# Layer 0 of a conditioned decoder step: one third of the conditioning projection ahead of the convolution, two thirds among its projections

## The chip, the cores and the metric

The kernel runs on one core of one Trainium2 chip. The time is device microseconds of one execution; each time shown is a median over the runs that are listed with it. The engines that matter here are PE (TensorE, matrix products), ACT (ScalarE), DVE (VectorE), POOL (GpSimd, which only issues transfers here) and SP (SyncE, which issues nearly all loads). They run their own instruction streams in order and meet at semaphores.

## What is computed

One inference step of a four-layer decoder trunk for 256 prompt tokens and 8 x 8 sample tokens (320 columns in all, model width 1024), all float32. Only layer 0 matters for the change:

```python
def adaln(c, w, b):
    mod = jax.nn.silu(c) @ w + b
    return jnp.split(mod[:, None, :], 6, axis=-1)

def modulate(x, g, shift, scale):
    return rms_norm(x, g) * (1 + scale) + shift
...
    sh1p, sc1p, g1p, sh2p, sc2p, g2p = adaln(c_prompt, ada_w[i], ada_b[i])
    hp = modulate(xp, norm1_g[i], sh1p, sc1p)
    yp, stp = conv_mixer(hp, ...)      # h @ w_in, a width-3 convolution with gates, @ w_out
    xp = xp + g1p * yp
    xp = xp + g2p * sq_relu_mlp(modulate(xp, norm2_g[i], sh2p, sc2p), mlp_w1[i], mlp_w2[i])
```

`ada_w` of a layer is 1024 x 6144. Its six blocks of 1024 columns are shift and scale of the first norm (sh1, sc1), the first gate (g1), shift and scale of the second norm (sh2, sc2) and the second gate (g2). The first norm needs sh1 and sc1 alone; g1 is needed when the convolution's output projection is added to x; sc2 and g2 are needed in the MLP. The other layers are windowed attention, pooling and latent attention over a paged cache, each followed by an MLP. Apart from y, the step returns the states, among them rolled copies of the attention windows (`out_swa_s`).

## The kernel before

Everything is written out by hand, engine by engine, with semaphores between them.

**Weights.** SP loads weight units of 1 MB (128 partitions x 2048 words) into a ring of four slots (`ring`, `load`, L421). Unit U may be loaded when unit U - 4 has been used (`unit_done`). For most phases each unit is split before use: ACT copies it to a rounded part `ring_hi` (`weights_hi`, L660, two halves), DVE subtracts to get the rest `ring_lo` in place (`weights_lo`, L1606), and PE runs three products per 128 x 128 block (hi x hi, hi x low of the input, low x hi). `conv_in` has 12 units of 48 such matmuls of 320 columns (L999); `conv_out` has 4 units of 16 plain float32 matmuls.

**The conditioning projection.** `ada_w` of a layer goes in three thirds r = 0, 1, 2 of eight units each. `ada_products(r, k)` (L1043) multiplies one unit by the 32 columns of `silu_c` into bank 5 or 6, in four matmuls of 512 columns; `ada_copy(r)` on ACT (L670) copies the bank out, `ada_turn(r)` on PE (L1052) transposes it with four matmuls into bank 7, and `ada_add(r)` on DVE (L1704) adds the bias and writes `mod`; `ada_scales` (L1713) turns the scale rows into (1 + scale) x gain. Third 0 holds sh1 and sc1, third 1 g1 and sh2, third 2 sc2 and g2. For layer 0 all 24 units come through the weight ring at the very start, ahead of the first norm. For layers 1 to 3 they come through a ring of their own of two slots (`ada_ring`, `ada_load`, L435), one unit behind each of 24 units of the MLP of the layer before.

**The first norm.** ACT squares x (L683), PE sums the squares with eight matmuls by ones into bank 4 (L1014), ACT takes the root (L685), DVE the reciprocal (L1577). Then for each pair of the eight chunks DVE multiplies (L1585) and treats the sample columns (L1593, L1594), ACT applies scale and shift to the prompt columns (L689) and makes `h_hi` (L695), DVE makes `h_lo` (L1581), and PE may start on that pair.

**The convolution.** The outputs of `conv_in` units 0 to 7 are copied out by ACT (L701). From unit 8 on DVE mixes: per chunk one group L1735 to L1749, eight chunks in all, 3.1 us each. PE waits for all eight (`conv_mixed`) before `conv_out`. DVE adds the output projection into x (L1612 to L1616, `mixer_update`), PE then turns the convolution's state (L961), ACT copies it out (L795) and goes on to the MLP.

**Rolled windows.** POOL issues 80 copies of up to 684 KB from `state_swa` to `out_swa_s`, DRAM to DRAM (`roll`, L326): 12 behind `conv_in`, 4 behind `conv_out`, 18 in layer 1, 8 + 16 in the projections and the prompt attention of layer 3, and 22 in the last MLP. The prompt attention's are each released by one head's products (`mlp_pv`).

Of the kernel before, what the change touches and what calls it, by code (L numbers as in the profile page):

```python
# [17 lines left out]
KD = D // P  # L18
# [29 lines left out]
NCH = {"ada": [0] * 24}  # L48
# [126 lines left out]
def build(nc, A, O):  # L175
    with ExitStack() as ctx:
# [237 lines left out]
        def _(sp):  # L414
# [12 lines left out]
            for u in range(24):  # L427
                load(u, u % RING, 1, SLOT, ada_rows_of(0, u // 8, u % 8), first=u < RING)

            def ada_load(l, x):  # L430

                y = 24 * (l - 1) + x
                if y >= 2:
                    sp.wait_ge(sem("ada_unit_done"), y - 1)
                sp.dma_start(ada_ring[:, x % 2, :].rearrange("p (k c) -> p k c", k=1), ada_rows_of(l, x // 8, x % 8))\  # L435
                  .then_inc(sem(f"ada_landed{x % 2}"), 16)

            def plain(phase, w, n, kc=KD, cols=256, col0=0):
                v = w.rearrange("(k p) n -> p k n", p=P)
                for u in range(n):  # L440
                    U = UNIT0[phase] + u
                    c = col0 + u * cols
                    width = min(cols, v.shape[2] - c)
                    load(U, U % RING, kc, width, v[:, :, c:c + width])

# [13 lines left out]
            plain("conv_in", A["conv_w_in"][0], 12)  # L459
            plain("conv_out", A["conv_w_out"][0], 4)  # L460
# [79 lines left out]
        def _(gp):  # L540
# [16 lines left out]
            roll_behind(0, "conv_in", 12)  # L557
            roll_behind(12, "conv_out", 4)
# [5 lines left out]
            roll_behind(16, "swa_qk", 12)  # L564
            roll_behind(28, "swa_v", 6)
# [25 lines left out]
            roll_behind(34, "mla_qa", 2)  # L591
            roll_behind(36, "mla_kva", 2)
            roll_behind(38, "mla_qb", 4)
# [4 lines left out]
            for i in range(16):  # L598
                gp.wait_ge(sem("mlp_pv"), i + 1)
                roll(42 + i)  # L600
# [17 lines left out]
        def _(act):  # L618
# [43 lines left out]
            def ada_copy(r):  # L662

                if r < 3:
                    act.wait_ge(sem("unit_done"), 8 * r + 8)
                else:
                    act.wait_ge(sem("ada_unit_done"), 8 * (r - 3) + 8)
                if r >= 2:
                    act.wait_ge(sem("ada_turned"), r - 1)
                act.activation(ada_rows[:, r % 2, :], bank[5 + r % 2][:, :], ACT.Copy).then_inc(sem("ada_copied"), 1)  # L670

            for r in range(3):
                ada_copy(r)
            weights_hi("conv_in", 0)
            weights_hi("conv_in", 1)

            def norm(ni, split=False):
# [7 lines left out]
                act.activation(rstd[:, 0, :], bank[4][:, 0:T], ACT.Sqrt, bias=tb("eps"), scale=1.0 / D).then_inc(sem("norm_std"), 1)  # L685
                for k in range(KD):
# [98 lines left out]
            norm(0, split=True)  # L785
# [5 lines left out]
            weights_hi("conv_in", 10)  # L791
            weights_hi("conv_in", 11)
            act.wait_ge(sem("conv_state_turned"), 1)
# [158 lines left out]
        def _(pe):  # L952
# [78 lines left out]
            def ada_products(r, k):  # L1031

                u = 8 * r + k
                if r < 3:
                    weights(u)
                    w = ring[:, u % RING, :]
                else:
                    pe.wait_ge(sem(f"ada_landed{k % 2}"), 16 * ((u - 24) // 2 + 1))
                    w = ada_ring[:, k % 2, :]
# [5 lines left out]
                mm.then_inc(sem("unit_done" if r < 3 else "ada_unit_done"), 1)  # L1045
# [78 lines left out]
            for r in range(3):  # L1124
                for k in range(KD):
                    ada_products(r, k)
                    if k == 2 and r:
                        ada_turn(r - 1)
            ada_turn(2)


            pe.wait_ge(sem("ada_read"), 5)
            norm(0, split=True)
            pairs("conv_in", 12, KD, ni=0)
            pe.wait_ge(sem("conv_mixed"), KD)
            pairs("conv_out", 4, KD, lambda k: cv_b[:, k, :])
            pe.wait_ge(sem("conv_state_ready"), 1)
# [428 lines left out]
        def _(dve):  # L1566
# [6 lines left out]
            def norm(ni, split=False):  # L1573
# [3 lines left out]
                own.link(dve.reciprocal(rstd[:, 0, :], rstd[:, 0, :]))  # L1577

# [128 lines left out]
            def ada_scales(l):  # L1707

                dve.wait_ge(sem("ada_read"), 3 * l + 5)
                for w in range(2):  # L1710
                    s = mod[:, mod_base(l, 3 * w + 1):mod_base(l, 3 * w + 1) + KD, :]
                    g = vcols((VEC_N2 if w else VEC_N1) + l * KD, KD).unsqueeze(2).to_broadcast([P, KD, 1 + NS])
                    ins = dve.scalar_tensor_tensor(s, s, 1.0, g, ALU.add, ALU.mult)  # L1713
                    own.link(ins) if w else own.mark(ins)
# [4 lines left out]
            for r in range(3):  # L1719
                ada_add(r)  # L1720
            ada_scales(0)


            weights_lo("conv_in", 0)
            weights_lo("conv_in", 1)
            norm(0, split=True)
            for u in range(2, 10):
                weights_lo("conv_in", u)
            for k in range(KD):
                if k in (2, 4):  # L1730
                    weights_lo("conv_in", 9 + k // 2)
                a = chunk_no("conv_in", 8 + k // 2, k % 2)
# [20 lines left out]
            mixer_update("conv_out", 0)  # L1753
            mlp(0)
# [341 lines left out]
```

## Time and profile before

| | us |
|---|---|
| median of three runs | 2438.51 |
| the three runs | 2429.34, 2438.51, 2442.95 |
| the profiled execution's own time | 2434.47 |
| its span | 2432.7 |
| PE busy in the span | 2135.9 (88%) |
| DVE busy | 1105.0 (45%) |
| ACT busy | 829.2 (34%) |
| read from HBM over the span | 392.01 MB |

The profile shows one execution. A row of the timeline gives start, duration, engine, line, operation, tile written and tiles read, shapes, and in brackets the idle time of the engine before it and what ended it. Lines are those of the kernel before; helpers such as `load` or `weights_hi` have one line for all their uses. A matmul of four-pass float32 shows as two records, so x8 under L1043 is one unit's four matmuls. PEclk is the granted TensorE clock as a share of 2.4 GHz.

### The profile page before, as it was taken

How to read it: one execution, taken by the hardware profiler on the slowest of the kernel's cores; microseconds unless marked ns; L12 is line 12 of the kernel's file. 1: busy time of each engine (PE TensorE's matmuls, PEld its weight loads, DVE VectorE, ACT ScalarE, POOL GpSimd, SP SyncE). 2: the span in 40 equal slices, each digit the busy share in tenths (PEclk: the TensorE clock that was granted, in tenths of full speed). 3: DMA queues.
4: the chain of work that ended last, by engine and by line, in shares of the span. 5: the costliest groups of instructions: out<-in, count | busy, mean ns of one | idle time of the engine just before them, and what ended most of it. 6: DMA issues, size and time to landing. Idle time of an engine off the chain costs nothing.

```text
span 2432.7 us, 33869 instructions
## 1 busy us (share of the span) xinstructions
PE 2135.9 (88%) x13570; PEld 1805.3 (74%) x13570; DVE 1105.0 (45%) x1760; ACT 829.2 (34%) x1445; POOL 54.0 (2%) x110
## 2 busy tenths in 40 slices
PE   4599799989968777999978999897899999889997
PEld 1297788879966555888867888863587777669997
DVE  1234554237815444553256542467533433335532
ACT  0230443135523332443224432343333333224421
POOL 0000000000010000000000000000100000000000
PEclk9799899999977898999989999997699999889999
DMA  7665377644560894477633776441501001026652
GB/s 281 256 228 197 133 246 263 217 141 170 203 216 24 238 280 127 156 248 263 201 98 122 246 263 224 146 165 61 183 20 44 22 22 43 1 69 225 242 212 74
DMA packets 230779, 399.45 MB, mean 164 GB/s; under 512 B 10184, under 2 KB 196335, under 8 KB 216689
## 3 DMA queue, kind: packets, MB, share of 16 engines
q1 hardware_dynamic: 224912, 332.69, 42.1%
q0 software_dynamic: 4576, 59.77, 6.3%
q10 hardware_dynamic: 1161, 5.11, 0.6%
q8 instruction: 100, 1.64, 0.3%
q14 instruction: 30, 0.25, 0.0%
HBM read 392.01 MB, written 59.76 MB: 186 GB/s over the span
## 4 chain that ended last, share of the span: by engine, by line
PE 77%; DVE 10%; DMA 6%; ACT 3%; issue 2%; SPq 1%; ACTq 0%; POOL 0%; DVEq 0%; POOLq 0%
PE bank L1069 37%; PE bank L999 11%; PE bank L1469 8%; PE bank L961 4%; PE bank L1043 3%; DVE rstd L1670 2%; PE bank L1161 2%; PE bank L1014 2%; DMA ring<-in_ada_w 2%; PE bank L1508 1%; PE bank L1478 1%; DMA work<-in_state_swa 1%; DMA ring<-in_mlp_w 1%; DVE hT L1585 1%; PE bank L1286 1%
## 5 line engine op out<-in xcount | busy, mean ns | idle before, releaser
L1606 DVE TENSOR_TENSOR ring_lo<-ring,ring_hi 128x1024 fp32r<-128x1024 f32 (+1 forms) x324 | 379.1, 1213 | 427.9 <-ACT ring_hi L660 427.8
L660 ACT ACTIVATE ring_hi<-ring 128x1024 fp32r<-128x1024 f32 (+1 forms) x324 | 322.8, 1046 | 452.2 <-PE bank L1069 185.8
L1069 PE MATMUL bank<-h_hi,ring_hi 128*128 128x320 f32 x1024 | 325.4, 318 | 27.8 <-DVE h_lo L1581 27.4
L1069 PE MATMUL bank<-hidden_hi,ring_hi 128*128 128x320 f32 x1024 | 322.9, 315 | 0.0
L1069 PE MATMUL bank<-h_lo,ring_hi 128*128 128x320 f32 x1024 | 319.2, 312 | 0.0
L1069 PE MATMUL bank<-hidden_lo,ring_hi 128*128 128x320 f32 x1024 | 318.5, 311 | 0.0
L1069 PE MATMUL bank<-h_hi,ring_lo 128*128 128x320 f32 x1024 | 318.5, 311 | 0.0
L1069 PE MATMUL bank<-hidden_hi,ring_lo 128*128 128x320 f32 x1024 | 318.5, 311 | 0.0
L961 PE MATMUL bank<-tab,work 128*128 128x128 f32 (+4 forms) x804 | 146.9, 323 | 116.8 <-DVE latents_lo L1992 17.5
L1069 PEld LDWEIGHTS bank<-h_hi,ring_hi 128*128 128x128 f32 x1024 | 195.2, 191 | 63.5 <-issue 60.7
L1069 PEld LDWEIGHTS bank<-hidden_hi,ring_hi 128*128 128x128 f32 x1024 | 194.6, 190 | 25.2 <-issue 25.2
L961 PEld LDWEIGHTS bank<-tab,work 128*128 128x128 f32 (+4 forms) x804 | 100.5, 158 | 151.5 <-issue 31.2
L1069 PEld LDWEIGHTS bank<-h_lo,ring_hi 128*128 128x128 f32 x1024 | 196.0, 191 | 0.0
L1069 PEld LDWEIGHTS bank<-h_hi,ring_lo 128*128 128x128 f32 x1024 | 195.4, 191 | 0.0
L1069 PEld LDWEIGHTS bank<-hidden_lo,ring_hi 128*128 128x128 f32 x1024 | 194.6, 190 | 0.0
L1069 PEld LDWEIGHTS bank<-hidden_hi,ring_lo 128*128 128x128 f32 x1024 | 194.3, 190 | 0.0
L1469 PE MATMUL bank<-ring_hi,latents_hi 128*128 128x512 f32 x512 | 172.7, 420 | 0.0
L999 PE MATMUL bank<-h_hi,ring_hi 128*128 128x320 f32 (+1 forms) x432 | 141.4, 327 | 20.6 <-DVE h_lo L1581 20.3
L1998 DVE TENSOR_REDUCE work<-work 128x8 f32<-128x1024 f32 x64 | 78.1, 1220 | 154.8 <-ACT work L909 154.8
L999 PE MATMUL bank<-h_lo,ring_hi 128*128 128x320 f32 (+1 forms) x432 | 136.9, 317 | 0.0
L999 PE MATMUL bank<-h_hi,ring_lo 128*128 128x320 f32 (+1 forms) x432 | 136.4, 316 | 0.0
L1642 DVE TENSOR_TENSOR work<-work x128 | 63.0, 492 | 141.5 <-ACT work L774 141.5
(242 smaller groups left out, 3075.4 us busy)
## 6 DMA issues: line engine op xcount, KB each, us to landing
ring<-in_mlp_w SPq DMA_DIRECT2D x128, 1024.0 KB, 7.6
work<-in_ada_w SPq DMA_DIRECT2D x72, 1024.0 KB, 5.2
out_swa_s<-in_state_swa POOLq DMA_DIRECT2D x40, 684.0 KB, 6.0
ring<-in_ada_w SPq DMA_DIRECT2D x24, 1024.0 KB, 8.8
work<-in_state_swa SPq DMA_DIRECT2D x80, 256.0 KB, 10.5
ring<-in_swa_w_qkv SPq DMA_DIRECT2D x18, 1024.0 KB, 6.6
work<-in_state_swa SPq DMA_DIRECT2D x16, 1024.0 KB, 9.8
out_swa_s<-in_state_swa POOLq DMA_DIRECT2D x24, 672.0 KB, 5.9
```

The source lines that it names most:

```text
L660: act.activation(ring_hi[:, place, part], ring[:, s, part], ACT.Copy).then_inc(sem("weights_hi"), 1)
L961: return pe.transpose(dst, src, ident[0:m, 0:m])
L999: mm = pe.matmul(bank[a % 4][0:m, 0:n], w[:, k, col:col + m], x(k), start=i == j == 0, stop=i == len(ks) - 1 and j == len(terms) - 1)
L1014: mm = pe.matmul(bank[4][:, 0:T], ones, hT[:, k, :], start=k == 0, stop=k == KD - 1)
L1043: mm = pe.matmul(bank[5 + r % 2][32 * j:32 * j + 32, :], silu_c[:, k, :], w[:, j * 512:(j + 1) * 512], start=k == 0, stop=k == KD - 1)
L1069: mm = pe.matmul(bank[a % 4][:, 0:T], w[:, k, :], x(k), start=first and k == 0 and j == 0, stop=last and k == KD - 1 and j == 2)
L1161: mm = pe.matmul(bank[a % 4][0:m, 0:256], x[:, k, t * P:t * P + m], w[:, k, :], start=k == j == 0, stop=k == KD - 1 and j == 2)
L1469: mm = pe.matmul(bank[2 * (x % 2) + i][:, :], lT_parts[y][:, c, x, :], kvb_parts[z][:, c, 512 * i:512 * (i + 1)], start=c == y == z == 0, ...
L1606: dve.tensor_tensor(ring_lo[:, s, part], ring[:, s, part], ring_hi[:, place, part], ALU.subtract)\
L1642: dve.tensor_tensor(raw, raw, raw, ALU.mult).then_inc(sem("hidden_squared"), 1)
L1670: own.link(dve.reciprocal(r, r))
L1998: dve.tensor_reduce(md_ss[:, j - 1, :], md_sq[:, :].rearrange("p (h d) -> p h d", h=H), AX_X, ALU.add)\
```

## The change

The first norm's squares and their sum go ahead of all conditioning products. Of the 24 conditioning units of layer 0 only the eight of third 0 still come through the weight ring at the start. The other sixteen come through `ada_ring`, and PE multiplies one behind each of the twelve `conv_in` units and two behind each of the first two `conv_out` units; `ada_turn(1)` stands behind unit 9 of `conv_in`, `ada_turn(2)` behind the last `conv_out` unit. On ACT the split of `conv_in` unit 0 stands ahead of `ada_copy(0)`, and that of unit 1 behind the norm instead of ahead of it; DVE follows suit. Sixteen rolled copies leave the convolution; all later ones move up, and sixteen are now issued in the decode part of layer 3, one behind every fourth page of keys (`md_keys`).

```diff
-NCH = {"ada": [0] * 24}
+NCH = {"ada": [0] * 8}
...
-            for u in range(24):
-                load(u, u % RING, 1, SLOT, ada_rows_of(0, u // 8, u % 8), first=u < RING)
+            for u in range(8):
+                load(u, u % RING, 1, SLOT, ada_rows_of(0, 0, u), first=u < RING)
...
-                y = 24 * (l - 1) + x
+                y = 24 * l + x - 8
                 if y >= 2:
                     sp.wait_ge(sem("ada_unit_done"), y - 1)
                 sp.dma_start(ada_ring[:, x % 2, :].rearrange("p (k c) -> p k c", k=1), ada_rows_of(l, x // 8, x % 8))\
...
-            def plain(phase, w, n, kc=KD, cols=256, col0=0):
+            def plain(phase, w, n, kc=KD, cols=256, col0=0, behind=lambda u: ()):
...
                     load(U, U % RING, kc, width, v[:, :, c:c + width])
+                    for x in behind(u):
+                        ada_load(0, x)
...
-            plain("conv_in", A["conv_w_in"][0], 12)
-            plain("conv_out", A["conv_w_out"][0], 4)
+            plain("conv_in", A["conv_w_in"][0], 12, behind=lambda u: (8 + u - 3,) if u >= 3 else ())
+            plain("conv_out", A["conv_w_out"][0], 4, behind=lambda u: ((17,), (18,), (19, 20), (21, 22, 23))[u])
...
-            roll_behind(0, "conv_in", 12)
-            roll_behind(12, "conv_out", 4)
...
-            roll_behind(16, "swa_qk", 12)
-            roll_behind(28, "swa_v", 6)
...
-            roll_behind(38, "mla_qb", 4)
+            roll_behind(18, "mla_qa", 2)
+            roll_behind(20, "mla_kva", 2)
...
             for i in range(16):
                 gp.wait_ge(sem("mlp_pv"), i + 1)
+                roll(26 + i)
+            for i in range(16):
+                gp.wait_ge(sem("md_keys"), 4 * i + 3)
                 roll(42 + i)
             roll_behind(58, "mlp1_3", 16)
             roll_behind(74, "mlp2_3", NS * len(ROLL) - 74)
...
-                if r < 3:
-                    act.wait_ge(sem("unit_done"), 8 * r + 8)
+                if r < 1:
+                    act.wait_ge(sem("unit_done"), 8)
                 else:
-                    act.wait_ge(sem("ada_unit_done"), 8 * (r - 3) + 8)
+                    act.wait_ge(sem("ada_unit_done"), 8 * r)
                 if r >= 2:
                     act.wait_ge(sem("ada_turned"), r - 1)
                 act.activation(ada_rows[:, r % 2, :], bank[5 + r % 2][:, :], ACT.Copy).then_inc(sem("ada_copied"), 1)
...
                 act.wait_ge(sem("norm_sum"), ni + 1)
                 act.activation(rstd[:, 0, :], bank[4][:, 0:T], ACT.Sqrt, bias=tb("eps"), scale=1.0 / D).then_inc(sem("norm_std"), 1)
+                if between:
+                    between()
...
-            norm(0, split=True)
+            def front():
+                weights_hi("conv_in", 0)
+                ada_copy(0)
+
+            norm(0, split=True, between=front)
+            weights_hi("conv_in", 1)
             for u in range(8):
                 for c in range(2):
                     k = 2 * u + c
                     copy_chunk("conv_in", u, c, (cv_b if k < KD else cv_c)[:, k % KD, :])
                 weights_hi("conv_in", u + 2)
             weights_hi("conv_in", 10)
+            ada_copy(1)
             weights_hi("conv_in", 11)
+            ada_copy(2)
             act.wait_ge(sem("conv_state_turned"), 1)
...
-                if r < 3:
+                if r < 1:
                     weights(u)
                     w = ring[:, u % RING, :]
                 else:
-                    pe.wait_ge(sem(f"ada_landed{k % 2}"), 16 * ((u - 24) // 2 + 1))
+                    pe.wait_ge(sem(f"ada_landed{k % 2}"), 16 * ((u - 8) // 2 + 1))
                     w = ada_ring[:, k % 2, :]
                 if k == 0 and r >= 2:
...
-                mm.then_inc(sem("unit_done" if r < 3 else "ada_unit_done"), 1)
...
-            for r in range(3):
-                for k in range(KD):
-                    ada_products(r, k)
-                    if k == 2 and r:
-                        ada_turn(r - 1)
-            ada_turn(2)
-
-
+            pe.wait_ge(sem("ada_read"), 2)
+            norm(0, split=True)
+            for k in range(KD):
+                ada_products(0, k)
+            ada_turn(0)
+
+            def ada_behind_in(u):
+                ada_products(1 + u // 8, u % 8)
+                if u == 9:
+                    ada_turn(1)
+
+            def ada_behind_out(u):
+                if u < 2:
+                    ada_products(2, 4 + 2 * u)
+                    ada_products(2, 5 + 2 * u)
+                if u == 3:
+                    ada_turn(2)
+
+            pairs("conv_in", 12, KD, ni=0, each=ada_behind_in)
+            pe.wait_ge(sem("conv_mixed"), KD)
+            pairs("conv_out", 4, KD, lambda k: cv_b[:, k, :], each=ada_behind_out)
+            pe.wait_ge(sem("conv_state_ready"), 1)
             pe.wait_ge(sem("ada_read"), 5)
-            norm(0, split=True)
-            pairs("conv_in", 12, KD, ni=0)
-            pe.wait_ge(sem("conv_mixed"), KD)
-            pairs("conv_out", 4, KD, lambda k: cv_b[:, k, :])
-            pe.wait_ge(sem("conv_state_ready"), 1)
...
                 dve.wait_ge(sem("norm_std"), ni + 1)
                 own.link(dve.reciprocal(rstd[:, 0, :], rstd[:, 0, :]))
+                if between:
+                    between()
...
-            for r in range(3):
-                ada_add(r)
-            ada_scales(0)
-
-
-            weights_lo("conv_in", 0)
+            def front():
+                weights_lo("conv_in", 0)
+                ada_add(0)
+                ada_scales(0, (0,))
+
+            norm(0, split=True, between=front)
             weights_lo("conv_in", 1)
-            norm(0, split=True)
             for u in range(2, 10):
                 weights_lo("conv_in", u)
             for k in range(KD):
                 if k in (2, 4):
                     weights_lo("conv_in", 9 + k // 2)
+                if k == 4:
+                    ada_add(1)
                 a = chunk_no("conv_in", 8 + k // 2, k % 2)
                 wait_read(dve, chunk_no("conv_in", 4 + k // 2, k % 2))
                 wait_chunk(dve, "conv_in", 8 + k // 2, k % 2)
...
             mixer_update("conv_out", 0)
+            ada_add(2)
+            ada_scales(0, (1,))
```

PE, from the end of the transposes of x (L968 in the changed kernel; lines shift by 7 on PE). Before, all conditioning products come first (the pattern runs on for 24 units):

```order
L961 MATMUL bank<-tab,work 128x64
L1043 MATMUL bank<-ring,silu_c 32x512 [waits x_ready,weights_landed0,x_copied,silu_ready]
L1043 MATMUL bank<-ring,silu_c 32x512 x3
L1043 MATMUL bank<-ring,silu_c 32x512 [waits weights_landed1]
L1043 MATMUL bank<-ring,silu_c 32x512 x3
```

In the changed kernel the sums of squares come first (L1021), then eight units (L1050), of which the last is shown, the transpose (L1059) and the first `conv_in` unit (L1006):

```order
L1021 MATMUL bank<-hT,tab 128x320 [waits ada_read,x_ready,squares,x_copied,silu_ready]
L1021 MATMUL bank<-hT,tab 128x320
...
L1050 MATMUL bank<-ring,silu_c 32x512 [waits weights_landed3]
L1050 MATMUL bank<-ring,silu_c 32x512 x3
L1059 MATMUL bank<-tab,work 128x36 [waits ada_read,ada_copied]
L1059 MATMUL bank<-tab,work 128x36 x3
L1006 MATMUL bank<-h_hi,ring_hi 128x320 [waits h_split,weights_split]
```

The sum moved past sixteen units that have left this place, and past eight that stay.

ACT of the changed kernel, from the squares to the split of `conv_in` unit 1 (L663 is `weights_hi`, L673 `ada_copy`, L689 and L695 the norm's first pair):

```order
L681 ACTIVATE hT<-xT 128x640 [waits x_ready] x4
L683 ACT_TABLE_LOAD
L683 ACTIVATE rstd<-bank,tab 128x320 [waits norm_sum]
L663 ACTIVATE ring_hi<-ring 128x1024 [waits unit_done,weights_landed0]
L663 ACTIVATE ring_hi<-ring 128x1024
L673 ACTIVATE work<-bank 128x512 [waits unit_done]
L689 ACTIVATE hT<-hT,mod 128x256 [waits normed]
...
L695 ACTIVATE h_hi<-hT 128x640 [waits h_sample,h_prompt]
L663 ACTIVATE ring_hi<-ring 128x1024 [waits unit_done,weights_landed1]
```

The copy of the third now stands behind the split of a weight unit; before it stood ahead of both splits.

SP of the changed kernel, from the start to the third conditioning unit in the convolution:

```order
L421 DMA ring<-in_ada_w 128x2048 x4
L421 DMA ring<-in_ada_w 128x2048 [waits unit_done] x4
L421 DMA ring<-in_conv_w_in 128x8x256 [waits unit_done] x4
L435 DMA work<-in_ada_w 128x2048
L421 DMA ring<-in_conv_w_in 128x8x256 [waits unit_done]
L435 DMA work<-in_ada_w 128x2048
L421 DMA ring<-in_conv_w_in 128x8x256 [waits unit_done]
L435 DMA work<-in_ada_w 128x2048 [waits ada_unit_done]
```

Each conditioning load stands right behind the load of the `conv_in` unit that waits for the fourth unit before it; before, the twelve `conv_in` loads followed one another.

## Rows read from the trace of the kernel before

**Rows 1.** The page: shares of the chain that ended last.
```profile
PE 77%; DVE 10%; DMA 6%; ACT 3%; issue 2%; SPq 1%; ACTq 0%; POOL 0%; DVEq 0%; POOLq 0%
```

**Rows 2.** Windows: length, busy time and instructions per engine, clock, DMA share, GB/s.
```profile
100.00:125.00 25.00, 18.13 (x68) 14.84 (x67) 10.98 (x18) 10.56 (x18) 0.00 (x1) 0.70 0.01 3
125.00:150.00 25.00, 25.00 (x172) 25.00 (x172) 9.45 (x8) 10.81 (x16) 2.02 (x4) 1.00 0.75 264
```

**Rows 3.** Timeline of the front, all engines: from the first product to `conv_in`.
```profile
33.91 6.49 PE L1043 MATMUL bank<-ring,silu_c 128*32 128x512 f32 x32 [0.79 <-DVE xT L1696]
...
50.54 1.93 PE L1043 MATMUL bank<-ring,silu_c 128*32 128x512 f32 x8 [1.56 <-DMA ring<-in_ada_w]
52.55 0.60 ACT L670 ACTIVATE work<-bank 128x512 f32<-128x512 f32 x1 [36.39 <-PE bank L1043]
...
83.98 90.39 SPq L421 DMA_DIRECT2D ring<-in_conv_w_in  x12
...
90.42 1.93 PE L1043 MATMUL bank<-ring,silu_c 128*32 128x512 f32 x8 [0.67 <-DMA ring<-in_ada_w]
...
93.07 1.92 PE L1052 MATMUL bank<-tab,work 128*128 128x36 f32 x8 [0.72 <-ACT work L670]
93.42 2.00 ACT L660 ACTIVATE ring_hi<-ring 128x1024 fp32r<-128x1024 f32 x2 [0.39 <-DMA ring<-in_conv_w_in]
95.03 0.31 DVE L1704 TENSOR_TENSOR mod<-bank,vec 128x144 f32<-128x144 f32 x1 [14.72 <-PE bank L1052]
...
98.34 2.60 ACT L683 ACTIVATE hT<-xT 128x640 f32<-128x640 f32 x4
...
99.20 7.20 PE L1014 MATMUL bank<-hT,tab 128*128 128x320 f32 x16 [4.20 <-ACT hT L683]
...
109.18 0.82 DVE L1585 TENSOR_TENSOR hT<-xT,rstd 128x640 f32<-128x640 f32 x1
...
112.93 0.60 PE L999 MATMUL bank<-h_hi,ring_hi 128*128 128x320 f32 x1 [6.53 <-DVE h_lo L1581]
```

**Rows 4.** Chain that ended last, layer 0's MLP: start, length, what.
```profile
296.04 1.00 PE bank L1043 x8
297.04 7.23 PE bank L1069 x48
...
436.89 1.01 PE bank L1052 x8
```

**Rows 5.** End of `conv_in` (POOL's copy behind its last unit), DVE's last chunk.
```profile
202.43 0.49 POOL L326 DMA_DIRECT2D out_swa_s<-in_state_swa  x1 [6.55 <-PE bank L999]
...
203.52 0.41 DVE L1735 TENSOR_TENSOR work<-work,bank 128x256 f32<-128x256 f32 x1
```

**Rows 6.** The same chain: all of `conv_out`.
```profile
206.63 36.41 PE bank L999 x128
```

**Rows 7.** DVE behind the first two chunks of `conv_out`.
```profile
212.94 0.48 DVE L1612 SCALAR_TENSOR_TENSOR xT<-bank,mod,xT 128x256 f32<-128x256 f32 x1 [6.14 <-PE bank L999]
...
217.24 0.48 DVE L1612 SCALAR_TENSOR_TENSOR xT<-bank,mod,xT 128x256 f32<-128x256 f32 x1 [3.43 <-PE bank L999]
```

**Rows 8.** SP's issues at 275 us and their landing (last number: us to landing).
```profile
274.95 0.37 SPq L421 DMA_DIRECT2D ring<-in_mlp_w  x1
275.36 0.58 SPq L435 DMA_DIRECT2D work<-in_ada_w  x1
...
ring<-in_mlp_w SPq DMA_DIRECT2D x1, 1024.0 KB, 5.7
work<-in_ada_w SPq DMA_DIRECT2D x1, 1024.0 KB, 7.7
```

**Rows 9.** The conditioning load issued at 243.49 us, with a rolled copy beside it.
```profile
work<-in_ada_w SPq DMA_DIRECT2D x1, 1024.0 KB, 10.5
```

**Rows 10.** DMA issues of layer 3's decode: the pages.
```profile
work<-in_cache_mla SPq DMA_DIRECT2D x64, 160.0 KB, 2.2
```

**Rows 11.** The window of the decode part of layer 3.
```profile
1760.00:2110.00 350.00, 330.06 (x1821) 271.84 (x1821) 138.95 (x222) 129.74 (x294) 0.00 (x0) 0.96 0.10 27
```

More of the change, by code:

```diff
@@ L561, in _ @@
             gp.dma_start(O["conv_s"].rearrange("a n r d -> (a n r) d"), cv_out[2:18, :]).then_inc(sem("conv_rows_stored"), 16)
-            roll_behind(16, "swa_qk", 12)
-            roll_behind(28, "swa_v", 6)
+            roll_behind(0, "swa_qk", 12)
+            roll_behind(12, "swa_v", 6)
             wait_banks(gp, "swa_out")
@@ L589, in _ @@
             gp.dma_start(O["pool_s"][0, :, HIST - SS:HIST], pl_out[0:TS, 1, :]).then_inc(sem("pool_rows_stored"), 16)
-            roll_behind(34, "mla_qa", 2)
-            roll_behind(36, "mla_kva", 2)
-            roll_behind(38, "mla_qb", 4)
+            roll_behind(18, "mla_qa", 2)
+            roll_behind(20, "mla_kva", 2)
+            roll_behind(22, "mla_qb", 4)
             gp.wait_ge(sem("latent_tok"), 3)
@@ L670, in ada_copy, with norm @@
                 act.activation(ada_rows[:, r % 2, :], bank[5 + r % 2][:, :], ACT.Copy).then_inc(sem("ada_copied"), 1)
-            for r in range(3):
[L673 to L677, printed above, removed]
+            def norm(ni, split=False, between=None):
                 l, w = ni // 2, ni % 2
@@ L1044, in ada_products @@
                                    start=k == 0, stop=k == KD - 1)
-                mm.then_inc(sem("unit_done" if r < 3 else "ada_unit_done"), 1)
+                mm.then_inc(sem("unit_done" if r < 1 else "ada_unit_done"), 1)
             def ada_turn(r):
@@ L1571, in seq, with norm @@
                 return ap.rearrange("p (n s) -> p n s", s=SS)
-            def norm(ni, split=False):
+            def norm(ni, split=False, between=None):
                 l, w = ni // 2, ni % 2
@@ L1705, in ada_add, with ada_scales @@
                    .then_inc(sem("ada_read"), 1)
-            def ada_scales(l):
-                dve.wait_ge(sem("ada_read"), 3 * l + 5)
-                for w in range(2):
+            def ada_scales(l, which=(0, 1)):
+                dve.wait_ge(sem("ada_read"), 3 * l + (5 if 1 in which else 3))
+                for w in which:
                     s = mod[:, mod_base(l, 3 * w + 1):mod_base(l, 3 * w + 1) + KD, :]
@@ L1713, in ada_scales @@
                     ins = dve.scalar_tensor_tensor(s, s, 1.0, g, ALU.add, ALU.mult)
-                    own.link(ins) if w else own.mark(ins)
+                    own.link(ins) if w == which[-1] else own.mark(ins)
                 if l == 2:
@@ L1717, in ada_scales @@
                     own.link(dve.tensor_tensor(g, g, vcols(VEC_POOL, KD).unsqueeze(2).to_broadcast([P, KD, 1 + NS]), ALU.mult))
-            for r in range(3):
-                ada_add(r)
-            ada_scales(0)
-            weights_lo("conv_in", 0)
+            def front():
[3 more added lines that the diff above has]
+            norm(0, split=True, between=front)
             weights_lo("conv_in", 1)
-            norm(0, split=True)
             for u in range(2, 10):
```

## The prediction

> **What bounds the kernel now.** Read the page's chain first [rows 1]: three quarters of the span end on PE, so the question for any stretch is whether PE works or waits. Then the windows [rows 2]. Between 125 and 150 us PE is busy without a gap at the full clock; between 100 and 125 us it is busy 18 of 25 us at a granted clock of 0.70, a mix of the 1.2 and the 2.4 GHz level, with the transfers idle. So the front is loose and the convolution is PE-bound. The front timeline [rows 3] says why. The first products begin at 33.91 us and take 6.49 us for the four units that have landed (x32 records, eight per unit); from then on PE waits for each 1 MB unit. The eighth unit starts at 50.54 us and the 24th at 90.42 us: sixteen units in 39.9 us, 2.49 us each, all of it transfer time. Behind them comes a serial piece of 22.5 us until the first `conv_in` matmul at 112.93 us: turn, bias, four splits on DVE, squares, sum, root, reciprocal, first pair of the norm.
>
> All times below are of the profiled execution (2434.47 us, span 2432.7); it lies 4.0 us, 0.17%, under the median of 2438.51 us. A measurement of this kernel can tell about 0.5% from no change (12.2 us); the three runs of before alone spread over 13.6 us.
>
> **The front.** I follow the new order with durations of before.
> - The squares need only x and an idle ACT: from 33.7 us on, the first pair done 0.65 us later (2.60 us for four) [rows 3]. PE's sum is eight float32 matmuls of 320 columns. At their old place they took 7.20 us in a stretch of clock 0.70 [rows 2, 3]; the same eight as a `conv_out` chunk take 217.24 - 212.94 = 4.30 us [rows 7]. Dense transposes run right ahead of the new place, and PE is idle for under 2 us in between, so I take 4.3 us; the other end is 7.2. The first product moves from 33.91 to 38.7 us: **4.8 us later**. Root and reciprocal lie beside products and transfers and cost nothing; what covers them is the wait for units 4 to 7.
> - Units 4 to 7 are released by the first products, so their landings move by the same 4.8 us: the eighth starts at 55.3 and ends at 57.2 us.
> - SP now has `conv_in` unit 0 behind the eighth. At the old end of the queue it landed 93.42 - 90.42 = 3.0 us behind the last conditioning unit [rows 3], so at 58.3 us. ACT splits it (2.00 us) before it copies the third (0.60 us): that order puts the copy at 60.4 instead of 57.3 us, a new wait of 3.1 us. Copy until 61.0; from the turn to the end of the bias row 95.03 + 0.31 - 93.07 = 2.3 us, and 0.4 us for one scale and its handoff: the norm's first multiplication can start at 63.8 us instead of 109.18 [rows 3]. **Gain 45.4 us**, and the first `conv_in` matmul moves from 112.93 to 67.5 us.
> - Unit 1's split now follows the norm on ACT: norm done near 72, ACT until 74.2, DVE until about 76 us. PE's unit 0 starts at 67.5 us, and it takes over 10 us as before, since it starts at the low clock behind single norm pairs; so this costs nothing.
>
> **The convolution.** In the MLP of layer 0 one unit with one conditioning unit behind it takes 1.00 + 7.23 = 8.23 us [rows 4]; a `conv_in` unit alone takes 7.04 us (the distance of POOL's copies, 6.55 idle + 0.49 [rows 5]). One conditioning unit so costs 1.19 us, a turn 1.01 us [rows 4]. Eleven stand between units of `conv_in`, with one turn: **+14.1 us**. The twelfth falls into the wait for DVE. That wait was 206.63 - 202.4 = 4.2 us, because DVE came to the last chunk at 203.52, 1.1 us late [rows 5, 6]; with PE slower by a sixth DVE keeps up and only its 3.1 us for the last chunk remain: **-1.1 us**. Four units in `conv_out` add 4.8 us. Behind it PE has a turn (1.0), and the state's transposes now wait for the bias of that turn (0.3, with 0.1 for the handoffs); ACT's state copies, the splits for the MLP and the second norm are queued behind: **+6.2 us** in all. The first chunk of `conv_out` took 6.3 us against 4.30 for the second [rows 6, 7], since PE had come out of 4.2 us of idleness at the low level; now a product unit shortens this idleness to 2 us. That saves between 0 and 2.0 us; I take **-1.0**.
>
> **The transfers beside it.** This is the place to look at hardest. The conditioning unit that PE needs behind `conv_in` unit j + 1 is loaded when unit j ends, behind a 1 MB weight load on the same queue. PE needs it one distance later, 8.23 us. Nearest row: such a pair, with nothing beside it, landed its second part 0.41 + 7.7 = 8.1 us after the first issue [rows 8]. That just fits; for scatter **+0.3 us**. With a rolled copy beside it the second part took 10.5 us [rows 9], 10.9 from the first issue; the change takes those copies away from here, so I stay with the row without one. Their removal gains nothing by itself: PE was already full [rows 2].
>
> The Trainium skill, "DMA: Bandwidth & Descriptors", section on the anatomy of one DMA, gives 2.0 us plus bytes at 436 GB/s per transfer; by that, as an estimate, the pair of 2 MiB would be there after 6.8 us, the slack would be 1.4 us and the +0.3 would be 0. The row's 8.1 us is the slower one and decides here.
>
> **The rolled copies.** Sixteen now run in layer 3's decode part, 350 us with a DMA share of 0.10 and 27 GB/s [rows 11]; a page lands in 2.2 us [rows 10] and is asked for about one sequence, some 40 us, ahead. Cost 0. Without that lead each could cost what a copy adds to a load (10.5 - 7.7 = 2.8 us [rows 8, 9]): at most 45 us.
>
> **Sum.** -45.4 + 14.1 - 1.1 + 6.2 - 1.0 + 0.3 = **-26.9 us**: the profiled execution would be 2408 us, the median 2411 us. Of 39.9 us of transfer taken out of the front, about 19 come back as PE time.
>
> **The rivals.**
> - *The conditioning loads pace the convolution, mildly.* If the pair lands after 9.3 us, near midway between the rows with and without a copy, each of eleven units waits 1.1 us: +12, so -15 and 2423 us. For it: the slack is 0.1 us, and only one unit of lead is left. Against: a good part of the present load there (DMA share 0.75 [rows 2]) is rolled copies, which go. Chance 0.13.
> - *The same, fully: slower than before.* It decides from a landing of 8.23 + 26.9/11 = 10.7 us on. The copy row's 10.9 is over it. `conv_in` unit 0, with others queued ahead, landed 93.42 - 83.98 = 9.4 us after its issue [rows 3]; with 2.49 us for a second transfer this is 11.9 us, 3.7 us late each time, +40 us, so +13 and 2452 us. Against: at 84 us the queue was several units deep, here it is empty each time. Chance 0.04.
> - *The rolled copies cost in the decode part.* If each of the sixteen delays PE by 1.9 us, two thirds of the bound above, the gain is gone (+3, 2442 us). PE is busy 330 of 350 us there [rows 11], so late pages would show in full; the lead speaks against. Chance 0.03.
> - *The front does not shrink as said*: the sum at the low clock (+2.9), and units 1 and 2 wait for splits that ACT now makes behind the norm, two of 2.0 + 1.2 us and a landing of 3 us bare, 9 us: -15, 2423 us. Chance 0.05.
> - *More than said*: `conv_out` starts at the full clock (-1.0), the order of split and copy costs nothing (-3.1), the start of `conv_in` is less broken up (-2): -33, 2405 us. Chance 0.09.
>
> **How the numbers follow.** The forecast has 0.66; its own range is 2403 to 2419 us (the terms' ends give -34 to -20, and the median of a few runs 2 us either way). Faster by over 0.5% means under 2426.3 us: the forecast, the better case, the mild pacing but for its worst part, most of the fourth: 0.88. Within 0.5%: 0.08. Slower: 0.04. The range from 2401 to 2425 us takes in the better case, the forecast and the milder half of the two cases at 2423, and leaves out the slow ones.
>
> **What would show it.** Right: the first `conv_in` matmul near 67.5 us; the sum of squares from 34.4 to 38.7 us; 8.2 us between ends of `conv_in` units; its end near 171, `conv_out` from 174 to 214 us; the decode part as long as before. Wrong: PE at L1050 waiting for `ada_w` for over 1 us per unit in `conv_in` (pacing); page loads over 2.2 us with PE waiting for them (rolled copies); ACT's split of unit 1 ending after PE's unit 0.

## The result, and the profile after

| | before | changed |
|---|---|---|
| median of eight runs each, us | 2440.70 | 2415.23 |
| lowest to highest | 2424.78 to 2448.17 | 2403.17 to 2422.02 |
| profiled execution, us | 2434.47 | 2403.17 |
| its span | 2432.7 | 2401.4 |
| PE busy | 2135.9 | 2124.0 |

The ratio is 0.990, with a 95% interval from 0.9873 to 0.9926: the medians differ by 25.5 us, and the interval allows 18 to 31 us. The forecast was 26.9 us, 2411 us, with a range from 2401 to 2425 us. The two profiled executions differ by 31.3 us; where the other 6 come from is told below, and they are not the change's.

The page of the changed kernel, its chain that ended last, reads as before [rows 1], with PE and ACT one point up each and transfers one point down:

```profile
span 2401.4 us, 33870 instructions
...
PE 78%; DVE 10%; DMA 5%; ACT 4%; issue 2%; SPq 1%; ACTq 0%; POOL 0%; DVEq 0%; POOLq 0%
```

The front of the changed kernel in its timeline (same columns as [rows 3], which it answers; L1021 is the sum, L1050 a conditioning unit, L1059 its turn, L1603 the norm's first multiplication, L1006 `conv_in`):

```profile
34.55 6.80 PE L1021 MATMUL bank<-hT,tab 128*128 128x320 f32 x16 [1.44 <-ACT hT L681]
...
41.28 3.64 PE L1050 MATMUL bank<-ring,silu_c 128*32 128x512 f32 x32
...
55.81 1.94 PE L1050 MATMUL bank<-ring,silu_c 128*32 128x512 f32 x8 [0.58 <-DMA ring<-in_ada_w]
58.80 2.00 ACT L663 ACTIVATE ring_hi<-ring 128x1024 fp32r<-128x1024 f32 x2 [16.88 <-DMA ring<-in_conv_w_in]
...
60.70 0.58 ACT L673 ACTIVATE work<-bank 128x512 f32<-128x512 f32 x1
...
61.33 1.93 PE L1059 MATMUL bank<-tab,work 128*128 128x36 f32 x8 [3.58 <-ACT work L673]
63.30 0.31 DVE L1722 TENSOR_TENSOR mod<-bank,vec 128x144 f32<-128x144 f32 x1 [0.97 <-PE bank L1059]
...
63.91 0.82 DVE L1603 TENSOR_TENSOR hT<-xT,rstd 128x640 f32<-128x640 f32 x1
...
67.65 0.61 PE L1006 MATMUL bank<-h_hi,ring_hi 128*128 128x320 f32 x1 [4.39 <-DVE h_lo L1599]
...
73.24 2.36 DVE L1624 TENSOR_TENSOR ring_lo<-ring,ring_hi 128x1024 fp32r<-128x1024 f32 x2
77.97 1.07 PE L1050 MATMUL bank<-work,silu_c 128*32 128x512 f32 x8
```

The norm starts at 63.91 instead of 109.18 us and `conv_in` at 67.65 instead of 112.93: 45.3 us. Unit 1's split on DVE is done at 75.60, before PE ends unit 0 at 77.97.

The chain through the convolution (start, length, what), which answers [rows 4 to 6]:

```profile
88.44 7.24 PE bank L1006 x48
95.68 0.99 PE bank L1050 x8
96.68 7.23 PE bank L1006 x48
...
120.81 8.59 DMA work<-in_ada_w
...
129.44 1.06 PE bank L1050 x8
...
175.64 10.55 PE bank L1006 x32
186.19 1.85 PE bank L1050 x16
188.05 8.81 PE bank L1006 x32
```

One unit with its conditioning unit takes 8.23 us. In three places PE waits for a conditioning load, for 1.11, 0.85 and 0.79 us; the second of them is for the load issued at 120.81. `conv_in` ends at 172.4 us (202.4 before [rows 5]), `conv_out` starts at 175.64 (206.63 [rows 6]). So 30 of the 45.3 us are left when `conv_in` ends, 31.0 at `conv_out`, and 25.4 at the sum of the second norm, which starts at 224.04 us instead of 249.48.

### The profile page after: what moved, and what is told of

The parts are those of the page before. It is cut to its first block, busy times and chain, and to the rows that moved or that the text cites. A ratio compares the mean times of both kernels' runs of the same rounds, so it can differ in the third digit from the quotient of the medians.

```text
span 2401.4 us, 33870 instructions
## 1 busy us (share of the span) xinstructions
PE 2124.0 (88%) x13570; PEld 1799.5 (75%) x13570; DVE 1105.6 (46%) x1760; ACT 828.5 (35%) x1445; POOL 54.0 (2%) x110
## 3 DMA queue, kind: packets, MB, share of 16 engines
HBM read 392.01 MB, written 59.76 MB: 188 GB/s over the span
## 4 chain that ended last, share of the span: by engine, by line
PE 78%; DVE 10%; DMA 5%; ACT 4%; issue 2%; SPq 1%; ACTq 0%; POOL 0%; DVEq 0%; POOLq 0%
PE bank L1076 37%; PE bank L1006 11%; PE bank L1485 8%; PE bank L968 4%; PE bank L1050 3%; DVE rstd L1688 2%; PE bank L1177 2%; PE bank L1021 2%; PE bank L1524 1%; PE bank L1494 1%; DMA work<-in_ada_w 1%; DMA ring<-in_mlp_w 1%; DVE hT L1603 1%; PE bank L1302 1%; PE bank L1496 1%
## 5 line engine op out<-in xcount | busy, mean ns | idle before, releaser
L663 ACT ACTIVATE ring_hi<-ring 128x1024 fp32r<-128x1024 f32 (+1 forms) x324 | 322.8, 1046 | 468.1 <-PE bank L1076 191.9
L968 PE MATMUL bank<-tab,work 128*128 128x128 f32 (+4 forms) x804 | 147.1, 324 | 116.3 <-DMA pages_sb<-in_page_table 14.9
L968 PEld LDWEIGHTS bank<-tab,work 128*128 128x128 f32 (+4 forms) x804 | 100.8, 159 | 151.6 <-issue 38.1
L1006 PE MATMUL bank<-h_hi,ring_hi 128*128 128x320 f32 (+1 forms) x432 | 142.4, 330 | 18.5 <-DVE h_lo L1599 18.2
L1006 PE MATMUL bank<-h_lo,ring_hi 128*128 128x320 f32 (+1 forms) x432 | 136.9, 317 | 0.0
L1006 PE MATMUL bank<-h_hi,ring_lo 128*128 128x320 f32 (+1 forms) x432 | 136.4, 316 | 0.0
```

The costliest lines, as they stand in the source:

```text
L663: act.activation(ring_hi[:, place, part], ring[:, s, part], ACT.Copy).then_inc(sem("weights_hi"), 1)
L968: return pe.transpose(dst, src, ident[0:m, 0:m])
L1006: mm = pe.matmul(bank[a % 4][0:m, 0:n], w[:, k, col:col + m], x(k), start=i == j == 0, stop=i == len(ks) - 1 and j == len(terms) - 1)
```

## The experiments

Each ran with the kernel before on the same chip; the ratio is to that kernel. Stretches are of each run's own profile.

| run | what is changed | ratio (95% interval) |
|---|---|---|
| changed kernel | | 0.990 (0.9873 to 0.9926) |
| e1 | rolled copies back behind the convolution | 0.9932 (0.9907 to 0.9957) |
| e2 | conditioning loads one unit earlier | 0.988 (0.985 to 0.991) |
| e3 | ACT's copy ahead of the split | 0.9881 (0.9859 to 0.9902) |
| e4 | four products ahead of the sum | 0.9875 (0.9848 to 0.9901) |
| e5 | kernel before, copies moved away | 0.9986 (0.9964 to 1.0008) |
| e6 | kernel before, sums ahead | 0.9981 (0.9959 to 1.0003) |
| e7 | e2, e4 and e9 together | 0.9862 (0.9834 to 0.989) |
| e8 | the two loads of a pair swapped | 0.99 (0.9865 to 0.9935) |
| e9 | e3, with DVE's order too | one run, 2408.28 us |
| e10 | one third in front; sums, copy and splits in their old order | 0.9909 (0.9875 to 0.9944) |

**e1, the rolled copies back.** In the changed kernel:

```diff
+            roll_behind(0, "conv_in", 12)
+            roll_behind(12, "conv_out", 4)
             gp.wait_ge(sem("conv_state_out"), 2)
...
                 gp.wait_ge(sem("mlp_pv"), i + 1)
-                roll(26 + i)
-            for i in range(16):
-                gp.wait_ge(sem("md_keys"), 4 * i + 3)
                 roll(42 + i)
```

The copies in between are numbered as in the kernel before.

> The changed kernel, with the sixteen rolled copies back behind the convolution's units, as before the change; all else is left. Theory (transfers pace the conditioning units once a copy runs beside them): the pair of loads lands 10.9 us after the first issue instead of 8.1 to 9.3, PE waits some 2.7 us at each of eleven conditioning units of conv_in, conv_in gets 25 to 30 us longer, and nearly the whole gain is gone: ratio to before 0.998 to 1.003. Rival (the landing has slack, the copies could have stayed): conv_in gets at most 5 us longer, ratio 0.990 to 0.993, and moving the copies was needless. Decode part of layer 3: same length either way.

`conv_in` from the end of unit 0 to that of unit 11 takes 107.3 us (78.12 to 185.46) instead of 94.4 (78.07 to 172.44): 13 us, half of what the theory said and well over its rival's 5. The time tells less: the ratio of 0.9932 lies below the theory's 0.998 and at the upper end of the rival's range, and its interval overlaps that of the changed kernel. First the landings between 75 and 170 us (last number), of the changed kernel:

```profile
work<-in_ada_w SPq DMA_DIRECT2D x12, 1024.0 KB, 7.8
ring<-in_conv_w_in SPq DMA_DIRECT2D x8, 1024.0 KB, 5.3
```

and of e1:

```profile
work<-in_ada_w SPq DMA_DIRECT2D x10, 1024.0 KB, 10.1
ring<-in_conv_w_in SPq DMA_DIRECT2D x8, 1024.0 KB, 6.8
```

The size of one landing was nearly right: 10.1 + 0.41 = 10.5 us from the first issue against 10.9 forecast. The number of waits was wrong. SP's timeline of e1 shows it; each row is the issue at the end of one unit:

```profile
78.12 0.37 SPq L421 DMA_DIRECT2D ring<-in_conv_w_in  x1
...
86.35 0.37 SPq L421 DMA_DIRECT2D ring<-in_conv_w_in  x1
...
98.45 0.37 SPq L421 DMA_DIRECT2D ring<-in_conv_w_in  x1
...
106.67 0.37 SPq L421 DMA_DIRECT2D ring<-in_conv_w_in  x1
```

The distances go 8.23, 12.10, 8.22. The pair for the next product is issued at a unit's end, before PE waits for the present one; so the wait is lead for the next pair, which then arrives in time. In all PE waited six times instead of eleven: 2.21, 2.57, 1.05, 1.22, 2.37 and 1.42 us, together 10.8 us against 2.75 us in the changed kernel. The rest of the 13 us is clock. Behind the first wait the granted clock was 0.50, the lower of its two levels; the products took 1.94 instead of 1.06 us and the next unit 7.95 instead of 7.23. The other two waits of over 2 us were followed by the same, which makes some 4.6 us for the three together; behind the three of 1.05 to 1.42 us the products took 1.07 us.

**e2, one unit of lead more.**

```diff
-            plain("conv_in", A["conv_w_in"][0], 12, behind=lambda u: (8 + u - 3,) if u >= 3 else ())
-            plain("conv_out", A["conv_w_out"][0], 4, behind=lambda u: ((17,), (18,), (19, 20), (21, 22, 23))[u])
+            plain("conv_in", A["conv_w_in"][0], 12, behind=lambda u: () if u < 3 else (8, 9) if u == 3 else (8 + u - 2,))
+            plain("conv_out", A["conv_w_out"][0], 4, behind=lambda u: ((18,), (19,), (20,), (21, 22, 23))[u])
```

> The changed kernel, with each conditioning load of the convolution issued one unit earlier (two loads behind conv_in unit 3, then one more ahead), so that PE has two units of lead instead of one. Theory (the three waits of about 1 us in conv_in are the pair landing later than 8.2 us): no wait for ada_w at the products behind conv_in, conv_in 3 us shorter, time 3 us less than the changed kernel, which the time alone cannot show. Rival (the waits come from the transfers' total rate, not from the lead): the waits stay or move to the ring weights, conv_in as long as now.

The theory holds. No product in `conv_in` waits for its weights; from the end of unit 0 to that of unit 11 it is 91.4 us (78.70 to 170.10) instead of 94.4; ten of the eleven distances are 8.2 us, the one with the turn is 9.1. The chain of e2, where the changed kernel has its first wait:

```profile
78.67 1.00 PE bank L1050 x8
79.67 7.24 PE bank L1006 x48
86.91 1.00 PE bank L1050 x8
87.91 7.23 PE bank L1006 x48
```

**e8, the order within the pair.** The conditioning load ahead of the weight load, at the same moment:

```diff
+                    if len(behind(u)) == 1:
+                        sp.wait_ge(sem("unit_done"), U - RING + 1)
+                        ada_load(0, behind(u)[0])
                     load(U, U % RING, kc, width, v[:, :, c:c + width])
-                    for x in behind(u):
-                        ada_load(0, x)
+                    if len(behind(u)) > 1:
+                        for x in behind(u):
+                            ada_load(0, x)
```

> The changed kernel, with the two loads behind each conv_in unit swapped in SP's queue (conditioning unit first, weight unit second), issued at the same moment as before. Theory (one queue serves them in order, the conditioning unit is late because the weight unit stands ahead of it): the conditioning unit lands after 5.2 us, as it does where the MLP issues it first, the weight unit after about 8; no wait at the products in conv_in, 3 us less than the changed kernel. Rival (the two share the engines evenly): both land after about 8 us in either order, the waits stay.

The waits are gone here too, with one unit of lead as in the changed kernel; from the end of unit 0 to that of unit 11 it is 91.4 us as in e2, and the ratio cannot show these 3 us. The landings of e8 between 75 and 170 us:

```profile
work<-in_ada_w SPq DMA_DIRECT2D x12, 1024.0 KB, 5.0
ring<-in_conv_w_in SPq DMA_DIRECT2D x8, 1024.0 KB, 7.5
```

5.0 and 7.5 us instead of 7.8 and 5.3: the load issued first is served first. The Trainium skill, "DMA: Bandwidth & Descriptors", section on queues, rings and completion order, says that a ring's descriptors are consumed in order; these two rows agree. So e1, e2 and e8 settle what the three waits are: a landing up to 1.1 us behind the need, because it stands behind a load that nobody is short of.

**e3 and e9, split and copy.**

```diff
             def front():
-                weights_hi("conv_in", 0)
                 ada_copy(0)
+                weights_hi("conv_in", 0)
```

> The changed kernel, with ACT copying the first third's products ahead of the split of conv_in unit 0, and DVE adding bias and scale ahead of its half of that split. Theory of the prediction (the order costs a wait of 3.1 us): the norm's first multiplication starts 3 us earlier, near 61 us. Rival (the landing of conv_in unit 0 at 58.8 us sets the end, the copy stood in its shadow): it starts only 1 to 1.6 us earlier, near 62.5 us, right behind DVE's half of the split.

This text speaks of DVE's order too; the kernel that ran had the lines above alone, and DVE's order was left. e9 then moved `weights_lo("conv_in", 0)` behind `ada_scales(0, (0,))` on DVE as well.

> The changed kernel, with the copy of the first third ahead of the split of conv_in unit 0 on ACT, and bias and scale ahead of DVE's half of it. The run e3 moved ACT's copy alone. Theory (the landing of conv_in unit 0 and its two-step split set the norm's start): first multiplication 3.4 to 3.6 us after that landing, 0.6 us better than e3's 4.05 us and 1.6 us better than the changed kernel's 5.1. Theory of the prediction (the order costs 3.1 us): 2.0 us after the landing.

From the landing of `conv_in` unit 0 (start of its split) to the norm's first multiplication it is 63.91 - 58.80 = 5.1 us in the changed kernel, 61.89 - 57.84 = 4.05 in e3, 62.49 - 59.02 = 3.47 in e9. The rival holds: what the order costs is 1.1 us (e3) to 1.6 us (e9, one execution), not 3.1. In e9 the copy is made at 57.76 and the scales are ready at 60.2, and DVE's split still holds the norm until 62.49. What sets the end is the landing and its two-step split.

**e4, products ahead of the sum.**

```diff
+            for k in range(RING):
+                ada_products(0, k)
             norm(0, split=True)
-            for k in range(KD):
+            for k in range(RING, KD):
                 ada_products(0, k)
```

> The changed kernel, with the products of the four landed conditioning units ahead of the sum of squares instead of behind it; the other four behind it. Theory (what the sum costs is that it holds back the release of the four ring slots): SP issues the fifth load at 36 us instead of 42.4, everything up to the norm moves 5 to 6.5 us ahead, first conv_in matmul near 62 us instead of 67.6; ratio to before 0.987 to 0.988. Rival (root and reciprocal then come too late, or the sum delays the fifth unit's products and with them conv_in unit 0's load): less than 3 us gained.

The theory holds. The chain of e4:

```profile
33.66 5.53 PE bank L1050 x32
39.19 4.50 PE bank L1021 x16
43.70 1.04 PE bank L1050 x8
```

The sum now lies in the wait for the fifth unit; `conv_in` unit 0 lands at 52.2 instead of 58.8 us, and the first `conv_in` matmul is at 61.03, 6.6 us earlier. The ratio, 0.9875, fits that and cannot be told from 0.990 by itself. (The second norm's sum starts 9.7 us earlier than in the changed kernel, at 214.37; 1.7 of these us are a first `conv_out` unit that came out at the full clock, see below.)

**e5 and e6, two parts of the change alone**, in the kernel before. e5 moves the rolled copies as the change does. e6 puts squares, sum, root and reciprocal ahead of all 24 units (`norm(0, split=True, between=front)` on ACT and DVE, with the three thirds and both splits in `front`).

> The kernel before, with one part of the change: the sixteen rolled copies leave the convolution, the later ones move up, sixteen run in the decode part of layer 3. Theory (the copies lay in cover at both places): no change, ratio 0.998 to 1.002, conv_in 7.04 us per unit as before, the decode part's key products as long as before (343 us from first to last). Rival (their removal frees PE or the ring in the convolution, so part of the gain is theirs): ratio 0.995 or less. Other rival (they slow the pages): over 1.003.

> The kernel before, with one part of the change: squares, sum, root and reciprocal of the first norm ahead of all 24 conditioning units, which all stay in front. Theory (the sum holds back the release of the ring's slots by 6.5 us, and what leaves the tail is the 8.7 us from the squares to the reciprocal): net 2 us gained, norm's first multiplication near 107 us instead of 109.2, not to be seen in the time (0.997 to 1.001). Rival (the sums ahead are a large part of the 45 us): 8 us or more gained, 0.996 or less, norm near 101 us.

e5: no change that can be told, as the theory said; its interval runs from 9 us faster to 2 us slower. The key products of the decode part (first and last start), before, changed and e5:

```profile
L1469 PEld LDWEIGHTS bank<-ring_hi,latents_hi x512: 186/188/338, 1763.5 to 2106.8; 128*128 128x128 f32 x171
```

```profile
L1485 PEld LDWEIGHTS bank<-ring_hi,latents_hi x512: 186/188/338, 1732.2 to 2075.6; 128*128 128x128 f32 x171
```

```profile
L1470 PEld LDWEIGHTS bank<-ring_hi,latents_hi x512: 186/188/338, 1768.9 to 2112.2; 128*128 128x128 f32 x171
```

343.3, 343.4 and 343.3 us: sixteen copies more in this part cost nothing there. From the first `conv_in` matmul to `conv_out` e5 takes 93.6 us (111.8 to 205.37), the kernel before 93.7, so the copies had not slowed PE in the old convolution either.

e6: 4.7 us, since `conv_in` starts at 108.22 instead of 112.93 us; more than the 2 expected, less than the rival's 8. The ratio, 0.9981, cannot be told from 1.

**e10, the short front with the sums at their old place.**

```diff
-            norm(0, split=True, between=front)
+            ada_copy(0)
+            weights_hi("conv_in", 0)
             weights_hi("conv_in", 1)
+            norm(0, split=True)
```

This is ACT. PE's `norm(0, split=True)` goes behind `ada_turn(0)`, and DVE's splits go behind its scales and ahead of the norm.

> The changed kernel, with the first norm's squares and sum at their old place behind the conditioning units and the splits of conv_in units 0 and 1; one third in front and two thirds beside the convolution as changed. It tells how the 45.3 us of the front divide. Theory (the eight units in front carry nearly all of it): norm's first multiplication near 69 us, 5 us later than in the changed kernel, first conv_in matmul near 73 us; ratio to before 0.990 to 0.993. Rival (only with the sums ahead does the short front pay): 10 us later or more, ratio 0.994 or over.

First multiplication at 68.81, first `conv_in` matmul at 72.55 us, ratio 0.9909. So of the 45.3 us of the front 40.4 come from the sixteen units that left. The other 4.9 are all of the new order together: the sums ahead and unit 1's split behind the norm, less what the split ahead of the copy costs (1.1 to 1.6 us by e3 and e9). e6, which moves only the sums in the kernel before, gives 4.7.

**e7, three of these edits together.** e2, e4 and e9 in one kernel.

> The changed kernel with the three edits of the runs before together: products of the four landed units ahead of the sum of squares, ACT's copy and DVE's bias and scale ahead of the split of conv_in unit 0, conditioning loads one unit earlier. Expected if they add: first conv_in matmul near 60 us (67.7 in the changed kernel), no wait for ada_w in conv_in, 10 us less than the changed kernel, ratio to before 0.984 to 0.987. If the ring weights or ACT become the bound of conv_in's first units: first matmul at 60 us but unit 1 waiting, and ratio 0.988.

First `conv_in` matmul at 59.76 us, 7.9 earlier than in the changed kernel; no wait in `conv_in`, which ends at 161.9 instead of 172.4 us. The ratio is 0.9862, the lowest of all, within the 0.984 to 0.987 expected, though its interval overlaps the changed kernel's. It cannot be told from e4 either, whose ratio is 0.9875 and whose median is 2408.5 us. The 10.5 us are in the trace; the medians of 2409.5 and 2415.2 us, taken on different occasions, show 6 of them, the two ratios 9. That e7 is faster than the changed kernel is likely, and not shown by the times.

## Why the prediction was right

*Front.* 45.4 us forecast, 45.3 measured; norm at 63.8, measured 63.91. That it agrees to 0.1 us is luck in part: two terms inside were off and stood against each other. The sum took 6.80, not 4.30 us, nearly the other end that was kept (5.94 to 7.39 us in the other runs that have it first). The four units behind it took 3.64 us, not the 6.49 of [rows 3], so the eighth unit started at 55.81 against 55.3. The step that failed here is "so I take 4.3 us", with its ground that dense transposes run right ahead. e4 puts the units first, and there they take 5.53 us and the sum 4.50: whatever comes first in this stretch runs slowly.

*Split ahead of copy.* Rightly carried through the sum, wrongly priced as a new wait of 3.1 us: most of the copy's delay stood in the shadow of a landing, and only 1.1 to 1.6 us of it could be had back (e3, e9).

*Convolution.* 8.23 us per unit forecast and measured; 1.19 us per conditioning unit is that less 7.04. Unit 0 took 10.4 us (67.65 to 78.07) where it took 12.1 before (112.93 to 125.00, where POOL issues its first copy behind `conv_in`). This 1.6 us was in no term of the sum; only the rival *More than said* named it, with 2 us. The wait for DVE is 175.64 - 172.42 = 3.2 us, forecast 3.1. The turn, the bias and the state's transposes behind `conv_out` came as forecast. The four units there cost 3.7 us, not 4.8, and the clock term was 0, not -1.0: the first unit took 10.55 us against 8.81 for the second. In e1 and e4, after the same idle time of 2.23 us, it took 8.88. So this term goes one way or the other from execution to execution, and what decides it was not found.

*Transfers.* Rightly named as the place to look; +0.3 forecast, 3.0 measured (94.4 against e2's 91.4 us), in three waits. Of all terms of the sum behind the front this is the one most mis-sized. The pair lands 8.2 us after the first issue in the middle, which is the need itself, and up to 9.3. The row at 8.1 us was one landing; its scatter was the term. The estimate from the figures of the Trainium skill, 6.8 us, was too low by 1.4; the skill gives them for a DMA on the software path, while the page of the profile has SP's loads on `q1 hardware_dynamic`.

*The slower rival* had the right mechanism and the wrong price. It charged each unit with a lateness; e1 shows 10.5 us landings costing 13 us, because a wait is lead for the next pair. By the same argument 11.9 us would not have cost 40; no run tried that.

*Rolled copies.* 0 forecast; in the decode part 0 measured (e5), in the whole time nothing that can be told. The move was still needed: with the copies in the convolution `conv_in` is 13 us longer, half of the gain (e1); the two ratios say a third, with intervals that overlap.

*Sum.* -45.3 in front, then 14.1 for the units and a turn, 2.8 of waits, -1.6 for unit 0, -1.0 at DVE's wait, 0.4 in `conv_out`'s own matmuls, 3.7 for its units and 1.5 behind it: -25.4 us at the second norm, forecast 26.9. So the two terms that were missed in `conv_in`, 2.5 us of waits and 1.6 us at unit 0, stood against each other too. That the medians say 25.5 is closer than their interval can promise. That the profiled pair shows 31.3 comes later, from pieces that take longer in one execution than in the other after idle stretches that both kernels have. Chain of the kernel before:

```profile
460.94 9.62 PE bank L1069 x48
...
535.30 7.62 PE bank L1014 x16
```

and of the changed kernel, the same two pieces:

```profile
434.74 8.85 PE bank L1076 x48
...
508.32 4.59 PE bank L1021 x16
```

The same sum of eight matmuls takes 7.62 us in one execution and 4.59 in the other, and nothing of the change is near: these two pieces are 3.8 of the 5.9 us. Pieces like these may also be part of why runs of the changed kernel spread over 19 us; this was not tried.

## What to carry to other kernels

If only a third of a projection is needed at first, it is worth loading alone: what lay bare as transfer came back as PE time at less than half (16 units: 39.9 us bare, 1.2 or less each beside other work). When a load is placed one step ahead of its use, compare its landing, counted from the first load in the queue at that moment, with the step's length; if they are equal, issue it one step earlier or put it ahead of the load that has slack. Before pricing a wait on one engine, look at whether a landing ends behind it anyway.

## What the runs showed of the hardware

The clock column can read full where matmuls run at half the rate. This is the changed kernel's sum, first in windows of 1 us (busy shares of the engines, and the granted clock as the third number from the end; the counts take in records that only reach into a window), then by PE's weight loads, one per record:

```profile
36.00:37.00 1.00, 1.00 (x3) 0.61 (x3) 0.00 (x0) 0.98 (x2) 0.00 (x0) 1.00 0.00 0
...
40.00:41.00 1.00, 1.00 (x6) 0.60 (x4) 0.00 (x0) 0.00 (x0) 0.00 (x0) 1.00 0.00 0
```

```profile
36.82 0.34 PEld L1021 LDWEIGHTS bank<-hT,tab 128*128 128x128 f32 x1 [0.20 <-issue]
37.35 0.34 PEld L1021 LDWEIGHTS bank<-hT,tab 128*128 128x128 f32 x1 [0.20 <-issue]
...
38.95 1.89 PEld L1021 LDWEIGHTS bank<-hT,tab 128*128 128x128 f32 x7 [0.20 <-issue]
```

Up to 38.95 us the records are 0.53 us apart, from there on 0.27, at a granted clock of 1.00 throughout. ACT had made the last square at 36.3 us (33.67 + 2.62), so PE was not waiting for input. Near the start of an execution the durations themselves are the better witness. What makes this stretch slow was not tried.

A late load can pay twice: in e1 three waits of 2.2 to 2.6 us were each followed by products of 1.87 to 1.94 instead of 1.06 us, at a granted clock of 0.50, and by a slower next unit, while the waits of 1.05 to 1.42 us, and those of up to 1.11 us in the changed kernel, were not. It is no rule: after 2.23 us of idleness `conv_out` started slowly in one execution and at the full clock in another.
